# Memory heads' sums as fp32r products with 24 filling steps ahead of the scores, and the first operations of a hybrid layer in another order

## What is computed

```python
h = rms_norm(x, attn_norm_g); proj = h @ w_in        # heads, gate columns b_raw/a_raw, z, mem_q, gates
beta = sigmoid(b_raw); g = -exp(dn_a_log) * softplus(a_raw + dn_dt_bias)      # 16 columns: "gate columns"
...                                                   # 8 attention heads, 8 delta-rule heads
o = rms_norm(o, dn_out_norm_g) * silu(z)              # delta-rule output, by head of 128
mem_k, mem_v = split(rms_norm(mem, mem_norm_g) @ w_mem_kv)
cq, ck = rms_norm(mem_q heads), rms_norm(mem_k heads) # 4 memory heads of 256
cp = softmax(cq @ ck.T / 16); mem_out = cp @ cv
x = x + sum(sigmoid(gate_raw) * (branches @ w_branch)) @ w_out
x = x + peer_ffn(rms_norm(x, ffn_norm_g), ...)        # 8 x 16 gathered expert rows for each token
```

## Time and profile before

| | us |
|---|---|
| median of 3 runs | 1212.28 |
| lowest, highest | 1211.66, 1216.48 |
| the profiled execution | 1212.86 |
| its span, from the first instruction to the last | 1211.1 |

### The profile page before, as it was taken

One profiled execution on the slowest core, in us unless ns is written; L12 is line 12 of the kernel. 1 busy time (PEld: TensorE's weight loads), 2 busy tenths in 40 slices (PEclk: granted clock), 3 DMA queues, 4 the chain that ended last, 5 costly groups with the idle time before them and its releaser, 6 DMA issues.

```text
span 1211.1 us, 17118 instructions
## 1 busy us (share of the span) xinstructions
PE 1077.0 (89%) x5253; PEld 742.5 (61%) x5253; DVE 722.8 (60%) x1726; ACT 528.0 (44%) x1045; POOL 618.8 (51%) x448
## 2 busy tenths in 40 slices
PE   8998999999999999999978879779788797887776
PEld 5878999999998999975524335234243252342232
DVE  5626666666653222236867666766676667666656
ACT  4555666666667776513332333233323332332221
POOL 3377776667774665832443444434344344344342
PEclk9999999999999999999999999999999999999999
DMA  7343333333332444966999999999999999999997
...
DMA packets 61157, 355.22 MB, mean 293 GB/s; under 512 B 7999, under 2 KB 8510, under 8 KB 27198
## 3 DMA queue, kind: packets, MB, share of 16 engines
...
HBM read 353.65 MB, written 1.05 MB: 293 GB/s over the span
## 4 chain that ended last, share of the span: by engine, by line
PE 54%; DMA 29%; issue 6%; ACT 5%; POOL 2%; DVE 2%; DVEq 0%; POOLq 0%; ACTq 0%; SPq 0%
DMA top<-peer_uv_dram,route 16%; PE ps L1973 12%; DMA front<-peer_uv_dram,route 11%; PE ps L1618 8%; PE ps L1619 8%; PE ps L1620 8%; PE ps L1939 4%; PE ps L1924 2%; PE ps L1784 2%; POOL split L962 2%; PE ps L1804 2%; DMA front<-branch_tiles_dram 1%; ACT top L899 1%; ACT split L582 1%; PE ps L1885 1%
## 5 line engine op out<-in xcount | busy, mean ns | idle before, releaser
L1973 PE MATMUL ps<-top 128*128 128x512 f32 x632 | 294.3, 604 | 86.8 <-ACT top L899 86.8
L962 POOL TENSOR_TENSOR split<-front,split 128x1024 fp32r<-128x1024 f32 x123 | 297.4, 2432 | 144.4 <-ACT split L582 144.2
L1012 POOL DMA_INDIRECT top<-peer_uv_dram,route x160 | 175.1, 1094 | 239.3 <-PE ps L1973 231.2
L1973 PEld LDWEIGHTS ps<-top 128*128 128x128 f32 x632 | 114.0, 189 | 254.6 <-ACT top L899 147.7
L1398 DVE CUSTOM_DVE_ANT_0 top<-top,scratch 128x1024 f32<-128x1024 f32 x160 | 195.9, 1225 | 118.4 <-DMA top<-peer_uv_dram,route 118.3
L1618 PE MATMUL ps<-split 128*128 128x256 f32 (+1 forms) x768 | 241.5, 314 | 6.2 <-POOL split L962 2.9
L1619 PE MATMUL ps<-split 128*128 128x256 f32 (+1 forms) x768 | 224.6, 292 | 0.0
L1620 PE MATMUL ps<-split 128*128 128x256 f32 (+1 forms) x768 | 224.6, 292 | 0.0
L899 ACT ACTIVATE top<-cst,route 128x128 f32<-128x128 f32 x254 | 88.1, 394 | 258.5 <-DVE route L1406 257.0
L582 ACT ACTIVATE split<-front 128x1024 fp32r<-128x1024 f32 x128 | 133.5, 1057 | 114.9 <-PE ps L1620 85.3
L1618 PEld LDWEIGHTS ps<-split 128*128 128x128 f32 x768 | 147.1, 191 | 13.7 <-issue 5.3
(11 more groups left out here) (298 smaller groups left out, 1575.8 us busy)
## 6 DMA issues: line engine op xcount, KB each, us to landing
...
```

What stands on the lines that cost most here:

```text
L962: pool.tensor_tensor(halves[slot(kind, i)][:, 1], raw[slot(kind, i)], halves[slot(kind, i)][:, 0], ALU.subtract).then_inc(lo_ready, 1)
L1012: pool.indirect_dma_start(rows_uv[k % RING], None, peer_uv, bass.IndirectOffsetOnAxis(ap=idx[c][:, k:k + 1], axis=0)).then_inc(s_row[k % R ...
L1973: ins = pe.matmul(ps[:, 2 * c + half, :], diag[:, k % 8, :], rows_uv[k % RING][:, D + half * 512:D + (half + 1) * 512], start=False, stop= ...
```

## The change

In the first microseconds:
- ACT takes a root of a zero as its first operation, before x is there.
- ACT squares only the first half of x; DVE squares the second, with its sum, in one operation.
- The gate columns are made in two halves of the contraction: the first right behind the transposes of x, in place of three idle products, the second where all of them stood.
- ACT copies the high parts of `hT` between the first three value tiles, not behind them. POOL's subtractions of tiles 1 and 2 wait until the first low half of `hT` is made.

In the memory heads:
- DVE adds the two halves of the squares twice, once rounded to fp32r and once in fp32, and subtracts. ACT squares the delta-rule heads twice, once rounded, and DVE subtracts. The sums are then two fp32r products each, of 512 columns. `mem_parts` holds DVE's four operations. They stand ahead of the wait for the head's last tile, for the next head. Their results lie in room of `squares` and in the rope tables, which are no longer in use.
- 24 steps, not 16, stand behind the sums. In the last head ACT's copy of branch tile 0 moves ahead of the copy of the transposed probabilities.

```diff
-        with nc.sbuf_tensor("squares", [P, 8 * T], F32R) as squares:
+        with nc.sbuf_tensor("squares", [P, AT_REST - AT_SCRATCH], F32R) as squares:
...
+        msq4 = msq.rearrange("p (a i t) -> p a i t", a=2, i=2)
+        mem_sq2 = [squares[:, at_sums + f * HT:at_sums + (f + 1) * HT] for f in range(2)]
+        head_sq2 = [tables[:, where[n][0]:where[n][0] + HT] for n in ("cos", "sin")]
...
-        MFILLS = (16, 12, 4)
+        MFILLS = (24, 12, 4)
...
-                for s in range(g * NC, (g + 1) * NC):
+                for s in (2, 3) if g else (0,):
                     if s:
-                        act.wait_ge(a_sq, s)
+                        act.wait_ge(a_sq, s - 1)
                     act.activation(junk, xin[:, s, :], ACT.Square, accum_out=ss4[:, s:s + 1]).then_inc(a_sq, 1)
...
+            act.wait_ge(s_zero, 1)
+            act.activation(root, zero[:, 0:1], ACT.Sqrt)
             norm_in(0)
...
-                act.activation(two(sqd), branch[:, 8 + 2 * m:10 + 2 * m, :], ACT.Square).then_inc(names["dn_sq"].sem, 1)
+                act.activation(two(sqd), branch[:, 8 + 2 * m:10 + 2 * m, :], ACT.Square)
+                act.activation(two(head_sq2[0]), branch[:, 8 + 2 * m:10 + 2 * m, :], ACT.Square).then_inc(names["dn_sq"].sem, 1)
...
-            for k in range(3):
-                high("mv", 0, k)
             for half in range(2):
+                high("mv", 0, half)
                 act.wait_ge(d_hT, 2 * half + 2)
                 act.activation(hT[:, 0, 4 * half:4 * half + 4], hraw[:, 4 * half:4 * half + 4], ACT.Copy).then_inc(s_hhi, 1)
+            high("mv", 0, 2)
...
                 ins.then_inc(names["probs"].sem, 1)
-                if not last:
+                if last:
+                    high("branch", 0, 0)
+                else:
                     high(*tile(4))
                     evacuate_mem(m + 1, 0, kind)
                 on(act, "p_turned", it)
                 copy("pT_ready", mpT, ps[:, 5, :])
                 if last:
-                    high("branch", 0, 0)
...
-            for k in range(3):
-                low("mv", 0, k)
+            low("mv", 0, 0)
+            pool.wait_ge(s_hlo, 1)
+            low("mv", 0, 1)
+            low("mv", 0, 2)
...
-                dve.wait_ge(a_sq, (g + 1) * NC)
+                if g:
+                    dve.wait_ge(a_sq, 3)
+                else:
+                    dve.wait_ge(s_x, 16 * NC)
+                    dve.tensor_tensor_reduce(out=hraw[:, 0:4, :].rearrange("p k t -> p (k t)"), in0=xin[:, 1, :], in1=xin[:, 1, :], scale=1.0,
+                                             scalar=0.0, op0=ALU.mult, op1=ALU.add, accum_out=ss4[:, 1:2]).then_inc(d_sq, 1)
+                    dve.wait_ge(d_sq, 1)
+                    dve.wait_ge(a_sq, 1)
...
+            def mem_parts(m):
+
+                it = HEADS + m
+                on(dve, "att_sq", it)
+                dve.tensor_tensor(two(mem_sq2[0]), msq4[:, :, 0, :], msq4[:, :, 1, :], ALU.add)
+                dve.tensor_tensor(msq4[:, :, 0, :], msq4[:, :, 0, :], msq4[:, :, 1, :], ALU.add).then_inc(done("mem_hi"), 1)
+                on(dve, "mem_hi", m)
+                dve.tensor_tensor(two(mem_sq2[1]), msq4[:, :, 0, :], two(mem_sq2[0]), ALU.subtract).then_inc(done("att_lo"), 1)
+                on(dve, "dn_sq", it)
+                dve.tensor_tensor(head_sq2[1], sqd, head_sq2[0], ALU.subtract).then_inc(done("dn_lo"), 1)
...
+                if m < MEM_HEADS - 1:
+                    mem_parts(m + 1)
                 dve.wait_ge(done("sig"), 1)
...
+            mem_parts(0)
             for m in range(MEM_HEADS):
                 mem_head(m)
...
-            idle_products(3)
-
-            def gate_rows():
-
-                pe.wait_ge(d_hT, 4)
+
+            def gate_rows(half):
+
+                pe.wait_ge(d_hT, 2 * half + 2)
                 pe.wait_ge(s_ba, 16)
-                for c in range(NC):
-                    for k in range(KT):
+                for k in range(4 * half, 4 * half + 4):
+                    for c in range(NC):
...
+            gate_rows(0)
...
-            gate_rows()
+            gate_rows(1)
...
-                on(pe, "att_sq", it)
-                for a in range(2):
-                    for i in range(2):
-                        ins = pe.matmul(ps[:, 3, a * T:(a + 1) * T], ones, msq[:, (2 * a + i) * T:(2 * a + i + 1) * T],
-                                        start=(i == 0), stop=(i == 1))
-                ins.then_inc(done("att_ss"), 1)
-                on(pe, "dn_sq", it)
+                on(pe, "att_lo", it)
+                pe.matmul(ps[:, 3, :], ones_r[:, :], mem_sq2[0], start=True, stop=False)
+                pe.matmul(ps[:, 3, :], ones_r[:, :], mem_sq2[1], start=False, stop=True).then_inc(done("att_ss"), 1)
+                on(pe, "dn_lo", it)
...
-                pe.matmul(ps[:, 6, :], ones, sqd, start=True, stop=True).then_inc(done("dn_ss"), 1)
+                pe.matmul(ps[:, 6, :], ones_r[:, :], head_sq2[0], start=True, stop=False)
+                pe.matmul(ps[:, 6, :], ones_r[:, :], head_sq2[1], start=False, stop=True).then_inc(done("dn_ss"), 1)
                 fill(MFILLS[0])
```

13 lines of the change are left out of this document (9 added, 4 removed).

## The result

| | before | after |
|---|---|---|
| median, 6 runs each (us) | 1214.6 | 1226.45 |
| lowest, highest | 1211.66, 1216.48 | 1223.36, 1229.73 |
| the profiled execution | 1212.86 | 1227.31 |
| its span | 1211.1 | 1225.5 |

The ratio is 1.0115, with a 95% interval of 1.010 to 1.0131. The prediction was 1216, with a range from 1208 to 1221. In the profiled executions the difference is 14.4 us.

A forecast was written before the change was run, and what follows sets the result against it. TensorE, busy for 89% of the span, was taken as the bound, with the DMA-fed last stage moving as a whole. Front -4.7, heads +5.0, clock spells +3.4 on 1212.86 gave 1216.6, 1216 against the median; range 1208 to 1221.

The forecast's parts named there:

- Front, -4.7: First microseconds: earlier start, shorter second column half and a removed clock slowdown give -6.4 us, or -4.7 with one new slowdown.
- The start (14.10): First microseconds: the first value product on TensorE was forecast to start at 13.95 us, against 16.91 before.
- the low half at its lower bound: First microseconds: DVE's first low half of the operand takes 1.2 to 3.1 us; 1.2 taken, ready at 13.8.
- the spell in front: Before the first value products: a possible stretch at the 1.2 GHz clock level, costing +1.7 us.
- Wait for tile 4, 2.5 us in heads 1 and 2: Memory heads, eight steps behind the scores: TensorE waits 2.5 us for POOL's low part of tile 4.
- Second wait, 1.4, for tile 5: Memory heads 1 and 2, behind the attention output: TensorE waits 1.4 us for tile 5.
- Spells, +3.4: Slow-clock stretches behind four new waits (heads 0 to 2, last head): between nothing and 6.8 us, two taken, +3.4.
- Rival (c): Memory heads and front: every new wait, and the columns in front, bring a 1.7 us clock loss; +8.8, 1221; chance 0.17.
- Head 0, -0.6: First memory head: loses its old scores wait, gains waits for tiles 3 and 5; ends at 407.0 against 407.54.
- Last head, +1.2: Last memory head (head 3): branch tile 0 comes before the transposes; branch tile 1 starts 1.2 us later.
- Sums, -1.7 a head: Memory heads: four fp32r products of 0.92 us replace fp32 sums of 2.6 us, -1.7 us per head on TensorE.
- (b): Memory heads: the fills do no harm; some -9 us there, -15 with the front, so 1198; chance 0.12.

## Why the prediction was wrong

Point by point, by its own steps:

- **Front, -4.7**: right. -4.6 in the trace, -5.1 by its own run. The start (14.10), the halves (1.94 and 1.85), the low half at its lower bound and the spell in front all came. That it was one spell is partly luck: of 16 executions with this front nine have one, five have two and two have none.
- **Wait for tile 4, 2.5 us in heads 1 and 2**: right, 2.54. **Second wait, 1.4, for tile 5**: the place was right; it measured 0.58 and 0.91. Without spells a head takes 31.9 us (in the kernel with eight more products) against the 31.7 worked out.
- **Spells, +3.4**: sized too small. The sum took two of four, "the middle". In the profiled execution three of its four waits had one (heads 1, 2 and the last); that for tile 3 in head 0 had none, and a fourth spell came behind the wait for tile 4 in head 0, which the sum didn't have. That is 6.8 where 3.4 stood. The prediction's caution was right, not every such wait brings a spell, but by all traces it is 16 of 21 behind waits of about 2.5 us and not one in two. Filling the waits is worth 8.4 us by the runs. That is more than the 6.8 of four spells, since head 2's wait for tile 0 went too and the branch stretch ran better. Rival (c), with 0.17, came nearest, but the rule that it names, a spell behind each wait, goes further than these runs, and its 1221 was still too low because of the next two terms.
- **Head 0, -0.6**: this step failed; measured +4.4. (Its own figures give 406.5 for the end of the head, not 407.0, so -1.0.) The working had the wait for tile 3 (2.23 us, 2.5 predicted) and then let tile 4 be in time. It was not: POOL's low part of it was held by VectorE's 2.28 us subtraction. The same collision stands in the trace before, where it was hidden, in rows that the prediction did not use (VectorE and POOL):

```profile
390.98 2.28 DVE L1288 TENSOR_TENSOR branch_lo<-branch_part,branch_hi 128x2048 fp32r<-128x2048 f32 x1
```
```profile
391.16 6.71 POOL L962 TENSOR_TENSOR split<-front,split 128x1024 fp32r<-128x1024 f32 x2 [2.10 <-ACT split L582]
```

  Two low parts alone are 4.7. After the change the wait was 3.35 us, and a spell stood behind it. Without the collision head 0 took 36.4, with a spell and a new wait of 1.38 us in it.
- **Last head, +1.2**: this step failed too; measured +6.4. Of this the spell is 1.7. The working followed TensorE to branch tile 1 and stopped there; it did not ask what late low parts do to the loads. They put off the next branch tile's load by 3.2 us (24.7 instead of 21.5 us into the head), ahead of a stretch in which the DMA engines are nearly full. That the eight steps of the last head cause it is shown by the runs with 16 and 24 there; that the late loads are the way is read from the traces, and no run takes them alone.
- **Sums, -1.7 a head**: the products did become shorter, but runs with the old sums took the same time, with 16 steps and with 24. This step failed as well: the prediction put the whole of it into TensorE's path; in the traces it turned into waits, for tile 0 right behind the sums (1.39 and 1.35, with 24 steps) or at the scores (1.11, with 16).

The range did not fail by the spells. It reached to 1221 "with all of them", six times 1.7 (the working lists five: four waits and the one in front, which give 1220), and the profiled execution had five. It failed by head 0 and the last head, for which it had no allowance beyond 3 us on the fast side: they missed by 3.3 and 3.5 us beside their spells (4.4 + 0.6 - 1.7 and 6.4 - 1.2 - 1.7). The wait for tile 0 in head 2 (1.35) is the next. One sum among the rivals is off as well: the -9 of (b) comes out as -10.9 from its own terms (four times 1.7, 2.37 and 1.7), and its -15 fits that.
